# Modulation chunks 8 to 19 of a two-block network: summed by VectorE in the stream, or by TensorE between the attention units

## What is computed

```python
for layer in range(DEPTH):
    shift, scale, gate = jnp.split((c @ mod_w[layer, 0] + mod_b[layer, 0])[:, None, :], 3, axis=-1)
    h = rms_norm(x, norm_w[layer, 0, 0]) * (1.0 + scale) + shift
    y = mixer_ab(h, ...)   # layer 0: projections, NSA and sliding-window attention, output product
    x = x + gate * rms_norm(y, norm_w[layer, 0, 1])
    shift, scale, gate = jnp.split((c @ mod_w[layer, 1] + mod_b[layer, 1])[:, None, :], 3, axis=-1)
    h = rms_norm(x, norm_w[layer, 1, 0]) * (1.0 + scale) + shift
    y = swiglu(h, ffn_w_in[layer], ffn_w_out[layer])
    x = x + gate * rms_norm(y, norm_w[layer, 1, 1])
```

## Time and profile before

| | |
|---|---|
| runs | median 1244.28 us of 3 (1243.93 to 1245.1) |
| the profiled execution | 1245.95 us, span 1244.1 us |
| busy in the span | PE 1150.2 us, DVE 933.0, ACT 584.8, POOL 74.5 |
| granted PE clock, mean | 0.967 of full speed |
| projections of the first mixer | PE works without a gap from 52 to 98 us |
| attention of the first mixer | p=0 begins on DVE at 100.81 us; PE's stage ends at about 158.8 |
| mod sums of DVE (L1361) | 168 in the program, mean 1285 ns |

### The profile page before, as it was taken

One profiled execution on the slowest core, in us unless ns is written; L12 is line 12 of the kernel. 1 busy time (PEld: TensorE's weight loads), 2 busy tenths in 40 slices (PEclk: granted clock), 3 DMA queues, 4 the chain that ended last, 5 costly groups with the idle time before them and its releaser, 6 DMA issues.

```text
span 1244.1 us, 19935 instructions
## 1 busy us (share of the span) xinstructions
PE 1150.2 (92%) x8342; PEld 1046.7 (84%) x8342; DVE 933.0 (75%) x1630; ACT 584.8 (47%) x960; POOL 74.5 (6%) x106
## 2 busy tenths in 40 slices
PE   2697898999998998899999999999989979999996
PEld 1695578999997996799999889999979967999996
DVE  5888858888776966788888688887666867765545
ACT  1434755443455457634444554444443355444433
POOL 1000000000000000186000000000000000000000
PEclk8799899999998998999999999999989999999999
DMA  9993234788982951477798447789622542765730
GB/s 374 360 381 139 117 136 179 305 328 280 336 317 100 379 213 41 148 288 263 310 261 333 184 178 289 284 245 353 263 107 97 109 178 101 265 249 193 180 131 34
DMA packets 40809, 280.75 MB, mean 226 GB/s; under 512 B 4736, under 2 KB 5264, under 8 KB 7952
## 3 DMA queue, kind: packets, MB, share of 16 engines
q1 hardware_dynamic: 37296, 269.27, 59.3%
q0 software_dynamic: 2416, 7.92, 2.1%
q10 hardware_dynamic: 1008, 2.30, 0.5%
HBM read 277.85 MB, written 1.10 MB: 224 GB/s over the span
## 4 chain that ended last, share of the span: by engine, by line
PE 68%; DVE 19%; DMA 6%; ACT 6%; issue 1%; ACTq 0%; SPq 0%; DVEq 0%
PE PS L413 68%; DMA raw<-WS 6%; DVE LO L1371 5%; DVE raw L1361 4%; ACT HI L952 2%; DVE TMP L1471 1%; DVE SC L1575 1%; ACT SQ L952 1%; DVE TMP L1436 1%; ACT HH L952 1%; ACT SC L952 1%; DVE SC L1560 1%; DVE HLo L1431 0%; PE PS L617 0%; DVE RS L1575 0%
## 5 line engine op out<-in xcount | busy, mean ns | idle before, releaser
L413 PE MATMUL PS<-HH,HI 128*128 128x256 f32 x1748 | 502.3, 287 | 27.7 <-ACT HH L952 24.9
L413 PE MATMUL PS<-HLo,HI 128*128 128x256 f32 x1748 | 503.9, 288 | 0.2
L413 PE MATMUL PS<-HH,LO 128*128 128x256 f32 x1748 | 500.5, 286 | 0.0
L1371 DVE TENSOR_TENSOR LO<-raw,HI 128x1024 fp32r<-128x1024 f32 x340 | 403.9, 1226 | 106.0 <-ACT HI L952 105.9
L952 ACT ACTIVATE HI<-raw 128x1024 fp32r<-128x1024 f32 x340 | 339.6, 1048 | 96.5 <-PE PS L413 58.7
L413 PEld LDWEIGHTS PS<-HH,HI 128*128 128x128 f32 x1748 | 341.2, 195 | 36.0 <-DVE LO L1371 20.5
L413 PEld LDWEIGHTS PS<-HH,LO 128*128 128x128 f32 x1748 | 341.1, 195 | 2.9
L413 PEld LDWEIGHTS PS<-HLo,HI 128*128 128x128 f32 x1748 | 340.5, 195 | 2.8 <-DVE HLo L1431 1.6
L1361 DVE CUSTOM_DVE_ANT_0 raw<-raw,CB,SM 128x1024 f32<-128x1024 f32 x168 | 210.6, 1285 | 23.1 <-DMA raw<-WS 23.0
L413 PE MATMUL PS<-HI,HDH 128*128 128x512 f32 x352 | 140.2, 398 | 0.0
L413 PE MATMUL PS<-HI,HDL 128*128 128x512 f32 x352 | 139.5, 396 | 0.0
(11 more groups left out here) (235 smaller groups left out, 1008.2 us busy)
## 6 DMA issues: line engine op xcount, KB each, us to landing
raw<-WS SPq DMA_DIRECT2D x255, 1024.0 KB, 5.3
SC<-scratch POOLq DMA_DIRECT2D x2, 1024.0 KB, 16.1
FB<-gates_out POOLq DMA_DIRECT2D x3, 512.0 KB, 5.1
SQ<-gates_out POOLq DMA_DIRECT2D x3, 512.0 KB, 9.6
X<-xT ACTq DMA_DIRECT2D x1, 1024.0 KB, 6.8
SC<-ssm POOLq DMA_DIRECT2D x2, 512.0 KB, 4.3
out<-TMP SPq DMA_DIRECT2D x2, 512.0 KB, 2.6
CB<-vecs SPq DMA_DIRECT2D x1, 512.0 KB, 6.5
```

Of the source, the lines that this page charges most:

```text
L413: return e.matmul(o, l, r, start=start, stop=stop, skip_group_check=True)
L1371: e.tensor_tensor(LO[:, s % HL, :], raw_half(j, h), HI[:, s % HL, :].bitcast(fp32), O.subtract).then_inc(*D.up(("lo", s)))
```

## The change

Chunks 8 to 19 become a fourth kind of chunk, "pm". They are laid out untransposed (128 rows of the contraction by 8 blocks of 256 columns), and PE sums them. In the stream they no longer stand between the ab chunks: the order is ab 0 to 7, the compression chunk, pm 8 to 19, abo. At each p from 0 to 5 PE takes a pair of chunks (`mod_rows`): per chunk 8 fp32 matmuls, whose weight is one column of c widened to 32 columns (a step of zero), whose moving side is one block of 256 columns, and which write to four groups of 32 partitions. ACT copies the bank to a row tile in `FB`. At the next p PE turns the rows into columns and adds the four groups, by four matmuls with the 128x128 row tile as weight and the one-column constant `sel` moving (`mod_turn`). DVE adds the bias and writes four columns of `MV`. The slot of a pm chunk is free when PE has used it. The small inputs get `cc` (8 columns), the constants `sel` (1 column). `walk.spare(2)` leaves the loop on all three engines. The gate vector of f0 is formed at p=7, not before the loop.

```diff
-    am = mods(4, 6)
-    plan += weave(ws("ab", 8), am[:7], 0) + [("raw", ("cmp", 0))] + am[7:] + ws("abo", 4)
+    plan += ws("ab", 8) + [("raw", ("cmp", 0))] + [("pm", ("pm", m)) for _, m in mods(4, 6)] + ws("abo", 4)
...
+        ROWS = [FB[:, 512 * i:512 * i + 512] for i in range(2)]
+        PAIRS = [(8 + 2 * i, 9 + 2 * i) for i in range(6)]
...
+            def mod_rows(n):
+                ps = take(("row", n))
+                for i, m in enumerate(PAIRS[n]):
+                    walk.weight(("pm", m), 0)
+                    j = where["pm", m]
+                    x = rawt[:, j % RAW, :].rearrange("p (k n) -> p k n", k=8)
+                    w.wait_ge(*loaded(j))
+                    for u in range(2):
+                        for g in range(4):
+                            k = 2 * g + u
+                            y = mm(ps[32 * g:32 * g + 32, i * 256:i * 256 + 256],
+                                   S("cc")[:, k:k + 1].to_broadcast([128, 32]), x[:, k, :], i == 0 and u == 0, u == 1)
+                    y.then_inc(*P.up(("pm", m)))
+                    walk.done(("pm", m), 0)
+                banks.give(("row", n))
+
+            def mod_turn(n):
+                ps = take(("pcol", n))
+                w.wait_ge(*A.at(("free", ("row", n))))
+                for t in range(4):
+                    x = mm(ps[:, t:t + 1], ROWS[n % 2][:, t * 128:t * 128 + 128], C("sel"), t == 0, True)
+                x.then_inc(*P.up(("pcol", n)))
+                banks.give(("pcol", n))
...
@@ PE, loop over p
-                walk.spare(2)
+                if 0 < p < 7:
+                    mod_turn(p - 1)
                 for f in compressed.get(p, ()):
                     f()
+                if p < 6:
+                    mod_rows(p)
...
@@ ACT, loop over p
-                high(walk.spare(2))
                 for f in compressed.get(p, ()):
                     f()
+                if p < 6:
+                    for m in PAIRS[p]:
+                        high(walk.weight(("pm", m), 0))
+                        walk.done(("pm", m), 0)
+                    w.wait_ge(*P.at(("pm", PAIRS[p][1])))
+                    if p > 1:
+                        w.wait_ge(*P.at(("pcol", p - 2)))
+                    fn(ROWS[p % 2], bank(("row", p)), F.Copy).then_inc(*A.up(("free", ("row", p))))
...
@@ DVE, before and in the loop over p
-            gate("f0", 16, 1.0, S("nw")[:, 8:16])
...
-                low(walk.spare(2))
                 for f in compressed.get(p, ()):
                     f()
+                if p < 6:
+                    for m in PAIRS[p]:
+                        low(walk.weight(("pm", m), 0))
+                        walk.done(("pm", m), 0)
+                if 0 < p < 7:
+                    c = 2 * PAIRS[p - 1][0]
+                    w.wait_ge(*P.at(("pcol", p - 1)))
+                    e.tensor_tensor(MV[:, c:c + 4], bank(("pcol", p - 1))[:, 0:4], S("mb")[:, c:c + 4], O.add) \
+                        .then_inc(*D.up(("free", ("pcol", p - 1)), ("col", c + 1), ("col", c + 3)))
+                if p == 7:
+                    gate("f0", 16, 1.0, S("nw")[:, 8:16])
...
@@ SP, before the load into the slot of chunk j - RAW
+                    elif kind == "pm":
+                        w.wait_ge(*P.at(key))
```

More of the change, by code:

```diff
@@ L15, in small_items @@
 def small_items():
-    return [("mb", 168), ("nw", 64), ("f1n", 8), ("mxn", 8), ("f2n", 8), ("fin", 8),
+    return [("mb", 168), ("cc", 8), ("nw", 64), ("f1n", 8), ("mxn", 8), ("f2n", 8), ("fin", 8),
             ("conv", 12), ("glub", 4), ("onc", 4), ("ons", 4), ("ssmd", 4), ("lre", 16), ("lim", 16), ("ldt", 16),
@@ L21, in const_items @@
 def const_items():
-    return [("ident", 128), ("ntri", 128), ("smask", 384), ("cmask", 15)]
+    return [("ident", 128), ("ntri", 128), ("smask", 384), ("cmask", 15), ("sel", 1)]
 def first_items():
@@ L165, in weight @@
         n = self.at_unit[j, half]
-        if self.plan[j][0] == "raw":
+        if self.plan[j][0] in ("raw", "pm"):
             return self.catch_up(n)
@@ L201, in build @@
     where = {p[1]: i for i, p in enumerate(plan) if p[0] != "mod"}
-    units = [(j, h) for j, p in enumerate(plan) for h in range(1 if p[0] == "raw" else 2)]
+    units = [(j, h) for j, p in enumerate(plan) for h in range(1 if p[0] in ("raw", "pm") else 2)]
     order = {u: n for n, u in enumerate(u for u in units if plan[u[0]][0] == "w")}
@@ L2126, in shape_constants @@
     put("ident", np.eye(128))
+    put("sel", (i[:, None] % 32 == 0).astype(np.float32))
     put("ntri", -(i[:, None] >= i[None, :]).astype(np.float32))
@@ L2199 @@
             a = tiles(f["glu_w_2"][0])
+        elif kind == "pm":
+            m = key[1]
+            a = fm(mod_w[m // 12][:, (m % 12) * 256:(m % 12) * 256 + 256])
         elif key[0] == "cmp":
@@ L2223 @@
     put("mb", np.concatenate([col(f["mod_b"]), col(f["b_mod_2"])], 1))
+    put("cc", col(f["c"][0]))
     put("nw", col(f["norm_w"]))
```

## The result

The change made the kernel slower: 1265.2 us (1264.1 to 1265.75, 4 runs) against 1244.69 of the kernel before beside it, ratio 1.0158 (95% interval 1.0145 to 1.0171); the medians are 20.5 us apart. They differ by up to 0.0007 from the quotient of the two medians.) The forecast was 1262, slower. The profiled execution has a span of 1263.9 us, 19.8 more than that of before.

What follows compares the result with a forecast made beforehand. PE bounds the projections; in attention PE and DVE hand over, neither full. Bias-start delays reach +15.9 at p=6, 0.2 more gives +16.1, clock 1.5: +17.6 on 1245.95 is 1263.5, or 1262 as median; range 1250 to 1275.

Steps and rivals of the forecast that it cites:

- What was free: Projections of the first block: about 14 of 24 removed DVE sums, 1.28 us each, are hidden because PE is full.
- the forecast's 0.8: Before attention: compression windows made early let DVE start p=0 at 100.0 in place of 100.8 us.
- The ring: At p=2, chunk 12 waits for the compression weights' slot; chunks 12 and 13 land 8.0 us (6.3 to 10) behind cmp_values.
- PE's order and the banks: p=1 to 6: scores(p+1) wait for DVE's add, next unit 1.1 us later; the first turn waits for ACT's copy.
- the list of takes: Walk of PE's four rotating PSUM banks: one bank of scores(p+1) is mod_turn(p-1)'s, freed by DVE's add.
- The prices: PE's added work: rows 2.1 us and turn 1.0 us per pair, 18.8 us for six; ACT's copies 0.60 us each.
- The clock, mis-sized: Behind the p=2 stall: PE's lower clock adds 0 to 3.5 us, taken as 1.5.
- A: Attention: all PE's added work is hidden in its idle time, at most -8.0 us, 1236 to 1241; chance 5%.
- B: Only the ring stall at p=2 counts, turn and rows lie beside DVE: 1247 to 1253; chance 13%.
- C: Rows' column groups do not overlap fourfold: two-way 1273, not at all 1290 to 1295; chance 14%.
- D: Attention loop: nothing to be seen, the stalls trade one for one; chance 3%.

Runs made afterwards that it cites:

- e1_ring: Changed kernel with the compression chunk three places later in the stream, so chunk 15, not 12, takes its slot: 1258.48 us, ratio 1.0102.
- e3_late: Changed kernel with each pair's turn moved behind values of its iteration and DVE's add behind the next bias work: 1274.03 us, ratio 1.0228.
- e2_ring_late: Changed kernel with the compression chunk three places later, the turn behind values and DVE's add behind the next bias work: 1267.91 us, ratio 1.0172.
- e8_ring_mid: Changed kernel with the compression chunk later in the stream and the turn right behind the compressed part, ahead of the next rows: 1258.19 us, ratio 1.0083.
- e11_mid: Changed kernel with only the turn moved behind the compressed part, compression chunk left in place: median 1264.76 us, ratio 1.0153.
- e7_dve8: Changed kernel with chunks 8 to 15 summed by DVE in the projections, 16 to 19 on PE, turns at p=1 and 2: 1246.75 us, ratio 0.9991.
- e5_onegroup: Changed kernel with a chunk's eight products all written to one group of 32 partitions in place of four: 1288.92 us, ratio 1.0335.
- e4_fill: Changed kernel with unneeded bf16 matmuls, 20 before the turn of pair 0 and 40 before the rows of p=2: 1263.08 us, ratio 1.0137.

## Why the prediction held, step by step

**What was free.** The 14 sums in the projections were hidden, as said. p=0 starts 2.0 us earlier. 0.7 of it is the forecast's 0.8, the windows made early: p=0 now starts 1.3 us behind the start of scores(0), before 2.0. The other 1.3 us are no gain of the change. The projections ended that much earlier in this execution because PE was at its upper level from 48 us on, where it was at the lower one before:

```profile
48.00:52.00 4.00, 4.00 (x22) 4.00 (x23) 4.00 (x5) 1.95 (x3) 0.00 (x0) 0.57 0.75 274
...
48.00:52.00 4.00, 3.90 (x32) 3.91 (x33) 4.00 (x5) 2.76 (x4) 0.00 (x0) 1.00 0.66 248
```

The first line is the kernel before, the second the changed one. e1_ring, the same program up to there, has the lower level in this stretch and p=0 at 100.60. The experiments show what these sums did cost: room in the stream, which did not bound the projections with eight chunks and did with ten.

**The ring.** Shown by e1_ring: 16.68 to 8.91 us. The step said 8.0 us from cmp_values to both chunks; the loads issued from 118.9 gave the first at 123.8 and the second at 126.2, 7.1 us behind cmp_values.

**PE's order and the banks.** The starts released by PE and the wait of the turn ahead of cmp_keys are in the profile. The bank itself weighed less than the forecast had it. One scores only, at 147.10, waits for DVE's add (0.61 us; DVE then stands 1.22 us for PE); at the others PE comes later than the add, so what releases DVE late is PE's work in front of scores, not the bank. Moving the turn takes 5.2 us off 1-2 in e3_late, e2_ring_late, e8_ring_mid and e11_mid. 2.1 of it is waiting (2.43 us became 0.35), 3.1 the clock that fell behind the wait. It does not come off whenever the turn is moved: in e7_dve8, with the same order, the clock fell and 1-2 is 9.36. And the first edit of mine that used the list of takes overlooked whom the freed bank goes to: the late turn cost 9 us more.

**The prices.** Rows 1.93 us (2.1 forecast), turn 1.05 (1.0), ACT's copy 0.60. The drains at a switch of tiling mode, of which TensorEngine Tiling (Array Packing) of the Trainium skill warns in its section Key Properties, show as no idle time in the profile: the rows at 143.55 follow the cmp_scores, and values follow the rows, with no gap. No run prices a drain alone.

**The clock, mis-sized.** This is the term that failed: I took 1.5 us. Against the full-clock durations, cmp_keys lost 1.24, the rows of p=1 1.71 and the scores behind 0.2; after the stall the second half of the rows of p=2 lost 0.9, scores 0.6, cmp_scores 0.5, the rows of p=3 1.71, values and scores together 1.0. That is 7.8 us, where 0 to 3.5 was allowed. It accounts for the excess at 1-2 (3.3 us) and at 3-4 (2.7), and at 2-3 it hid that the chunks came 0.9 us sooner than forecast. The earlier p=0 (1.2 us, mostly the clock before 52 us), the quicker ring (0.9) and the cheaper work of the other steps took back some 3.4 of the 6.3 that were missing, and so 1262 stood beside 1265.2. The sign, the ring stall and PE's added work on the path are shown; that 1262 is so close is in part luck, errors that cancelled.

**The rivals.** A fails on the 7.1 us behind cmp_values, B on e1_ring, which is still at 1.0102 with the stall gone, C on the 1.93 us of a pair and on e5_onegroup. D fails on the time. What stays open is what brings PE's clock down in this loop. Where the turn waited 2.4 us ahead of cmp_keys they ran slow (3.29 us, and 3.62 in e1_ring), and where that wait was gone or filled they took 2.05; but e1_ring and e4_fill show the clock falling later behind waits of 0.24 us or less.

## What to carry to other kernels

Work that lies under a full engine cost nothing here as long as the stream had room for its data; moving it to an engine that hands over to others in a loop puts it, and the waits of its hand-overs, on the path. Before a consumer is moved ahead in program order, ask which ring slot and which PSUM bank it takes, who frees them, and who takes them next: both can be counted from the program. If an engine does have room, put the first half of the work where its data is long there and the second where nobody waits for it; with two pairs left on PE that placement took 0.9991 to 0.9968, and the larger step was to leave eight of the twelve chunks on the engine whose time was hidden: 0.9991, where ring and order mended alone gave 1.0083.

## What the runs showed of the hardware that was not expected

The slow clock, 0.50 to 0.68 over 4 to 8 us, came at a different place of the loop in nearly every kernel: behind waits of 0.2 to 5.1 us, and once (e4_fill, from 107 us) with hardly a gap on PE since 98. The same wait of 0.35 us ahead of the first turn was followed by the slow clock in e7_dve8 and by the full one in e8_ring_mid. It nearly doubles what is issued in it: 1.93 to 3.64 us for a pair of rows. In this loop 3 to 8 us hang on it, as much as on some of the edits. The first of five chunks issued within 2 us landed after 4.8 us here and after 7.3 before. Before, POOL's row of 512 KB was moving beside it; no run shows that this is the cause.
